# Attention steps rebuilt: head norm's inverse root on POOL, scaling behind the next squares, new order at group changes and ends

## The reference, cut to what matters

```python
def sliding_window_attention(h, positions, w_in, q_gain, k_gain, sinks, w_out):
    q, k, v = split(h @ w_in)                  # 16 heads of q, 4 of k and v, head size 64
    q = rope(rmsnorm(q, q_gain), positions)    # mean square over the 64 of a head, + 1e-6
    k = rope(rmsnorm(k, k_gain), positions)
    # blocks of 128 queries; keys of the block before and of its own
    scores = einsum("bnqkgd,bnskd->bnkgqs", q, k) * 64 ** -0.5
    scores = where(band of 128, scores, -inf)
    probs = softmax(concat([scores, sink]))[..., :-1]
    o = einsum("bnkgqs,bnskd->bnqkgd", probs, v)
    return o @ w_out
```

## Time and profile before

| | us |
|---|---|
| median of 3 runs | 2653.89 |
| lowest, highest | 2653.49, 2654.97 |
| the profiled execution, device time | 2654.76 |
| its span in the trace | 2653.1 |
| TensorE busy | 2569.6 (97%) |
| VectorE busy | 1771.6 (67%) |
| ScalarE busy | 927.8 (35%) |
| POOL busy | 278.2 (10%) |

### The profile page before, as it was taken

How to read it: one execution, slowest core, us unless ns; L and a number is a source line. 1 busy time by engine, 2 the same in 40 slices (tenths; PEclk the granted TensorE clock), 3 DMA queues, 4 the chain that set the end, 5 groups by cost and what they waited for, 6 DMA issues and landing times.

```text
span 2653.1 us, 36828 instructions
## 1 busy us (share of the span) xinstructions
PE 2569.6 (97%) x11929; PEld 2145.0 (81%) x11929; DVE 1771.6 (67%) x3397; ACT 927.8 (35%) x1732; POOL 278.2 (10%) x344
## 2 busy tenths in 40 slices
PE   8999999999999999999999978988999999999999
PEld 6888878888788888888888867877877888888887
DVE  6545454454577876667766777888878666667765
ACT  5332332323311544442111255545554444311112
POOL 2102011020000300000000052322330000000000
PEclk9999999999999999999999999999999999999999
DMA  6012120121433333353233201001023323532332
GB/s 202 31 51 69 48 74 14 48 72 48 143 96 99 123 116 123 103 177 124 95 96 101 82 21 41 17 24 40 17 76 115 127 96 110 206 96 95 95 97 85
DMA packets 161729, 231.67 MB, mean 87 GB/s; under 512 B 21681, under 2 KB 103889, under 8 KB 161618
## 3 DMA queue, kind: packets, MB, share of 16 engines
q1 hardware_dynamic: 159314, 226.10, 26.5%
q10 hardware_dynamic: 2304, 4.20, 0.4%
HBM read 171.53 MB, written 58.73 MB: 87 GB/s over the span
## 4 chain that ended last, share of the span: by engine, by line
PE 80%; DVE 10%; issue 5%; ACT 4%; DMA 1%; POOL 0%; SPq 0%; DVEq 0%; ACTq 0%; POOLq 0%
PE ps L480 26%; PE ps L482 26%; PE ps L481 26%; ACT xn L1936 2%; DVE smax L1982 1%; DVE hss L2015 1%; DVE pT_lo L1960 1%; PE ps L1362 0%; PE ps L1313 0%; PE ps L1345 0%; DVE xT L659 0%; PE ps L1315 0%; PE ps L1314 0%; DVE ws_lo L1806 0%; DVE hT_lo L531 0%
## 5 line engine op out<-in xcount | busy, mean ns | idle before, releaser
L659 DVE TENSOR_TENSOR xT<-ps,xT 128x512 f32<-128x512 f32 x704 | 482.2, 689 | 264.1 <-PE ps L482 263.9
L480 PE MATMUL ps<-aT_hi,wd_hi 128*128 128x512 f32 x1408 | 554.0, 393 | 23.6 <-DVE xT L659 19.6
L482 PE MATMUL ps<-aT_hi,wd_lo 128*128 128x512 f32 x1408 | 550.3, 391 | 0.0
L481 PE MATMUL ps<-aT_lo,wd_hi 128*128 128x512 f32 x1408 | 550.0, 391 | 0.0
L480 PE MATMUL ps<-bh,uw_hi 128*128 128x512 f32 x880 | 343.7, 391 | 6.8 <-DVE xn L857 6.0
L481 PE MATMUL ps<-bl,uw_hi 128*128 128x512 f32 x880 | 343.3, 390 | 0.0
L482 PE MATMUL ps<-bh,uw_lo 128*128 128x512 f32 x880 | 343.1, 390 | 0.0
L480 PEld LDWEIGHTS ps<-aT_hi,wd_hi 128*128 128x128 f32 x1408 | 265.5, 189 | 78.7 <-DVE xT L659 14.4
L482 PEld LDWEIGHTS ps<-aT_hi,wd_lo 128*128 128x128 f32 x1408 | 265.4, 189 | 55.9
L481 PEld LDWEIGHTS ps<-aT_lo,wd_hi 128*128 128x128 f32 x1408 | 265.8, 189 | 53.7
L442 ACT ACTIVATE aT_hi<-raw 128x1024 fp32r<-128x1024 f32 x80 | 80.6, 1052 | 595.7 <-PE ps L482 580.7
(11 more groups left out here) (287 smaller groups left out, 4649.0 us busy)
## 6 DMA issues: line engine op xcount, KB each, us to landing
raw<-in_w_up SPq DMA_DIRECT2D x64, 512.0 KB, 5.6
raw<-in_w_down SPq DMA_DIRECT2D x64, 512.0 KB, 3.6
raw<-a_dram SPq DMA_DIRECT2D x64, 512.0 KB, 3.3
raw<-in_ret_w_in SPq DMA_DIRECT2D x48, 512.0 KB, 5.0
a_dram<-upost SPq DMA_DIRECT2D x64, 256.0 KB, 2.1
a_dram<-xn SPq DMA_DIRECT2D x64, 256.0 KB, 2.0
xT<-x_dram SPq DMA_DIRECT2D x24, 512.0 KB, 6.0
y_dram<-xn SPq DMA_DIRECT2D x32, 256.0 KB, 2.3
```

The costliest lines, as they stand in the source:

```text
L480: pe.matmul(bank, ah, bh, start=(begin and i == 0), stop=False, skip_group_check=not begin)
L481: pe.matmul(bank, ah, bl, start=False, stop=False, skip_group_check=not begin)
L482: last = pe.matmul(bank, al, bh, start=False, stop=(i == len(pairs) - 1), skip_group_check=not begin)
L659: dve.tensor_tensor(xT[:, k, cols], ps[:, banks[m % len(banks)], :], xT[:, k, cols], ALU.add).then_inc(x_add, 1)
```

## The change

It has six parts.

1. The head norm's inverse root: VectorE works out the seed in one operation (L479); the refinement, ten operations on 128x5 (`rsqrt_rest`), runs on POOL between the gains and the rotation. The constant factors are folded into the scale of the mean. VectorE's scaling of the heads waits for the tenth; the maxima and the sink stand behind it. All other inverse roots have eight operations for nine.
2. `prob_act` has lag 2 instead of 1 and stands behind `sq_act`.
3. The turn: TensorE runs f0 and f1 ahead of a; VectorE's two additions of the turn come first in it; b of a group's last block waits for them (`ahead = 2`). In the step before the turn the additions and masks are mixed with the splits, and all stand ahead of the scaling.
4. The start: one tile of the down projection fewer is left between the steps, a of the first block waits for the norm's low parts piece by piece, POOL adds its norm parts elsewhere.
5. The end: in the drain ScalarE scales block 6 first, and the edges of the norm (`b_hi_act`, `edge_low`) all stand in the drain.
6. The inverse root of the last norm's second half stands ahead of a split of MLP weights instead of behind it (`plain_dve`, with `p_hi_act` to match), and that of the attention's norm is worked out between other work in step 3 of group 0.

```diff
-RSQ = 9
+RSQ = 8
+REST = 10
+HSCALE = (256 / 3) ** 2
+HCONST = (3.0, 20 / 3, 320 / 9)
...
+        def rsqrt_seed(dve, a, r):
+            return dve.tensor_scalar(r.bitcast(I32), a.bitcast(I32), -0.5, float(0x5F3759DF), ALU.mult, ALU.add)
+
+        def rsqrt_rest(pool, count, base, a, r, t):
+            def step(k, ins):
+                ins.then_inc(count, 1)
+                pool.wait_ge(count, base + k + 1)
+            step(0, pool.tensor_tensor(t, r, r, ALU.mult))
+            step(1, pool.tensor_tensor(t, t, a, ALU.mult))
+            step(2, pool.tensor_tensor(t, hconst[:, 0, :], t, ALU.subtract))
+            step(3, pool.tensor_tensor(r, t, r, ALU.mult))
...
+            step(9, pool.tensor_tensor(r, t, r, ALU.mult))
...
-        FILLED = TILES - 3
+        FILLED = TILES - 2
...
             if layer == 1:
-                p_lo_dve(dve, layer, 7)
                 norm_rstd(dve, 3, 0)
             for kk in range(4):
                 t_dve(dve, layer, 6, kk)
+            if layer == 1:
+                p_lo_dve(dve, layer, 7)
...
+            if isinstance(g, int) and i == 0:
+                for k in range(KT):
+                    pe.wait_ge(n_lo, TILES + k + 1)
+                    last = product(pe, ps[:, SA, 0:SW_COLS], pairs[k:k + 1], begin=k == 0)
...
+            ahead = 2 if t == TT - 1 and not (isinstance(g, int) and g == SW_KV - 1) else 0
             if not isinstance(i, int) or i > 5:
-                pe.wait_ge(x_add, TILES * DG_SW + 2 * (i - 5))
+                pe.wait_ge(x_add, TILES * DG_SW + 2 * (i - 5) + ahead)
...
             pool.tensor_tensor(qk_raw[:], qk_raw[:], qkgain[:], ALU.mult).then_inc(sw_gain, 1)
+            pool.wait_ge(sw_var, 3 * (i + 1))
+            rsqrt_rest(pool, sw_rsq, REST * i, hvar[:], hrs[:], htmp[:])
...
         def drain_act(act, s):
             if s == TT:
+                prob_act(act, LAST, TT - 2)
...
-                for t in (2, 3):
+                for m in (4, 5):
+                    add(dve, DG_SW + LAST, m, BDS)
+                for t in range(4):
                     edge_low(dve, 1, t)
                 p_lo_dve(dve, 1, 0)
-                for m in (4, 5):
-                    add(dve, DG_SW + LAST, m, BDS)
...
                     if turn:
                         run(lambda *a: f_pe(*a, 0), g, s, FLAG)
+                        run(lambda *a: f_pe(*a, 1), g, s, FLAG)
                     a_pe(eng, g, s)
...
                     sq_act(eng, g, s)
+                    run(prob_act, g, s, 2)
                     run(qkT_act, g, s, 1)
...
                     run(oT_act, g, s, 2)
-                    run(prob_act, g, s, 1)
...
-                        work = lows(g, s) + splits[:2] + masks[:2] + splits[2:] + masks[2:]
+                        work = lows(g, s) + outs[:1] + scores[:2] + splits[:1] + outs[1:] + splits[1:]
+                        outs = []
                     else:
-                        work = lows(g, s) + masks
-                    scale_dve(eng, g, s, work)
-                    for w in out_adds(g, s):
+                        work = lows(g, s) + scores[:2]
+                    for w in work:
                         w()
+                    scale_dve(eng, g, s)
+                    for w in scores[2:] + outs:
+                        w()
```

More of the change, by code:

```diff
@@ L461, in step @@
                 dve.wait_ge(count, base + k + 1)
[L463 to L467, removed]
-            c = math.sqrt(3 / 8)
@@ L470, in rsqrt @@
[L470 to L473, removed]
+            step(0, rsqrt_seed(dve, a, r))
+            step(1, dve.scalar_tensor_tensor(t, r, -0.5, r, ALU.mult, ALU.mult))
+            step(2, dve.tensor_tensor(t, t, a, ALU.mult))
+            step(3, dve.scalar_tensor_tensor(r, t, 1.5, r, ALU.add, ALU.mult))
@@ L1037, in plain_act @@
                 h12_act(act, layer, kk, final)
[L1038 to L1045, removed]
+            for i in (5, 6):
+                for kk in range(4):
+                    b_hi_act(act, layer, i, kk, final)
+            p_hi_act(act, layer, 7)
             for s in range(3):
@@ L1816, in a_pe @@
                     pe.wait_ge(x_add, TILES * DG_SW - 3)
-            if isinstance(g, int) and g == 0 and t % 4 == 0:
-                hT_ready(pe, t // 4)
+            if isinstance(g, int) and g == 0 and t == 4:
+                hT_ready(pe, 1)
             wait(pe, sw_vlo, i)
-            product(pe, ps[:, SA, 0:SW_COLS],
-                    [(hT_hi[:, k, t * P:(t + 1) * P], hT_lo[:, k, t * P:(t + 1) * P], ws_hi[:, k, :], ws_lo[:, k, :])
-                     for k in range(KT)]).then_inc(a_mm, 1)
+            pairs = [(hT_hi[:, k, t * P:(t + 1) * P], hT_lo[:, k, t * P:(t + 1) * P], ws_hi[:, k, :], ws_lo[:, k, :])
+                     for k in range(KT)]
+            if isinstance(g, int) and i == 0:
+                for k in range(KT):
+                    pe.wait_ge(n_lo, TILES + k + 1)
+                    last = product(pe, ps[:, SA, 0:SW_COLS], pairs[k:k + 1], begin=k == 0)
+                last.then_inc(a_mm, 1)
+            else:
+                product(pe, ps[:, SA, 0:SW_COLS], pairs).then_inc(a_mm, 1)
         def b_pe(pe, g, t):
@@ L2131, in drain_act @@
             if s == TT:
+                prob_act(act, LAST, TT - 2)
                 qkT_act(act, LAST, TT - 1)
                 pT_act(act, LAST, TT - 2)
-                for kk in (2, 3):
+                act.wait_ge(a_mm, TT * SW_KV)
+                for kk in range(4):
                     b_hi_act(act, 1, 1, kk, SW_FINAL)
@@ L2240, in step @@
                     run(c_pe, g, s, 1)
-                    run(lambda *a: f_pe(*a, 1), g, s, FLAG)
+                    if not turn:
+                        run(lambda *a: f_pe(*a, 1), g, s, FLAG)
                     run(e_pe, g, s, 2)
@@ L2264, in step @@
                     run(oT_act, g, s, 2)
-                    run(prob_act, g, s, 1)
                     if begins and s == 1:
-                        for m in (FILLED + 1, FILLED + 2):
+                        for m in (FILLED, FILLED + 1):
                             last_norm_act(eng, m)
[L2269 to L2272, removed]
                 if which == "dve":
-                    if begins and s == 1:
-                        fill_dve(eng, FILLED)
+                    outs = out_adds(g, s)
+                    if turn:
+                        for w in outs:
+                            w()
+                        outs = []
                     run(qkT_dve, g, s, 1)
@@ L2298, in step @@
                     if begins and s < 3:
-                        for m in ((8, 9, 10), (11, 12), (13, 14, 15))[s]:
+                        for m in ((8, 9, 10), (11, 12, 13), (14, 15))[s]:
                             norm_low(eng, m)
-                    if begins and s == 3:
-                        norm_rstd(eng, 2, 1)
-                    if last_group and s == TT - 1:
-                        for m in range(2):
-                            edge_low(eng, 1, m)
                 if which == "pool":
                     rope_sw_pool(eng, g, s)
-                    if begins and s < 2:
-                        norm_pool(eng, 2, 1, ((3,), (4, 5, 6, 7))[s])
+                    if begins and s == 1:
+                        norm_pool(eng, 2, 1, (6, 7))
             def group(g, last_group):
@@ L2573, in _ @@
                 pool.memset(flat if z is kr else flat.bitcast(F32), 0.0).then_inc(sw_zero, 1)
+            for j, c in enumerate(HCONST):
+                pool.memset(hconst[:, j, :], c).then_inc(sw_zero, 1)
             norm_pool(pool, 2, 0)
-            norm_pool(pool, 2, 1, (1, 2))
+            norm_pool(pool, 2, 1, (1, 2, 3, 4, 5))
             sw_steps("pool", pool)
```

42 lines of the change are left out of this document (30 added, 12 removed).

## The result

The changed kernel took 2673.49 us in the median of 4 runs (2672.24 to 2675.66), the kernel before 2653.99 (2653.49 to 2654.97, 4 runs): ratio 1.0074, 95% interval 1.0056 to 1.0091. It is slower by 19.5 us. The profiled execution took 2672.24 us with a span of 2670.6, which is 17.5 us more than the span before.

A forecast was written before the change was run, and what follows sets the result against it. Two loops, TensorE's and one through VectorE and ScalarE, both turned at 11.35 us a step. Terms 1.9 + 21.3 - 8.1 + 3 - 5 = +13.1 on 2654.76, less 0.87, gave 2667 us; range 2651 to 2687.

The forecast's parts named there:

- Steady step: Seven of a group's eight steps: 12.3 us each, 0.93 more; +21.3 us over 21 steps of groups 1 to 3.
- the second loop: Loop through VectorE and ScalarE, vp_lo to vp_lo: 9.3 us plus POOL's chain, 12.3 us; TensorE's loop is the other, 12.2.
- POOL's price: Ten small head-norm operations in a row on POOL: 3.0 us taken, ends 2.6 and 3.8.
- Turn: Three turns between groups: vp_lo to vp_lo falls from 20.71 to 18.0 us, b starting at 16.0; -8.1 us for three.
- Start: Kernel start together with group 0's steps (+5.5 us): +1.9 us.
- -3.6: Start without group 0's steps: the 2.9 us wait for hT_lo goes and a(0) gains some 0.7 us.
- Drain: After the last vp_lo: late maxima lengthen VectorE's chain, last d at 26.2 us instead of 24.2; +3 us, ends +1 and +4.5.
- Last norm: Behind the attention: inverse root fits into VectorE's idle 4.36 us ahead of the split, all behind comes sooner; -5 us.
- Hidden scaling: Rival: ScalarE's scaling ends beside b, so d is not held; steps stay 11.36 us, total 2640 us; chance 0.12.
- Turns close: Rival: b never waits, TensorE keeps full clock, turns under 15 us; total 2652 us, half of it 2659; chance 0.14.
- Slow POOL: Rival: POOL's chain in each step takes 3.8 us, steps 13.0 us; total about 2686 us; chance 0.17.
- stretched case: POOL's chain stretched by 1.7 beside VectorE's work to 5 us, giving 2710 us.

The follow-up runs named there:

- the kernel without the two edits: Changed kernel with the root back on VectorE, its operations one by one between other work, and ScalarE's scaling back at the step's end: 2639.87 us.

## Why the prediction was right, and where it was off

- **Steady step, right, with two sizes off that cancelled.** d came 1.46 us behind a's end (1.43 said), steps took 12.25 us (12.3), 21.4 us in all (21.3). With the scaling put back the second loop alone gave 12.68 us for 12.7 worked out, and with the root put back the first alone 12.21. On VectorE sdif's end at 6.84 us behind vp_lo met the 6.8 by luck: the chain took 2.68 us where the sum has 3.0, so L2056 came 0.3 us sooner than said, and the three small operations took 0.71 us, from 1899.22 to 1899.93, where the sum has 0.4. The 21.4 us too hold one step of 13.80 (see the end) that no term forecast.
- **POOL's price, right at its lower end.** 0.20 us for 128x5 is the value of the line through the larger shapes, and 2.68 us for the chain lies near the 2.6 of the range. No operation of the chain was stretched: in all 32 blocks it took 2.67 to 2.72 us, beside P^T's low halves, masks and additions. The splits of weights, which the rule in the prediction names, stood behind it and never met it. What was stretched is VectorE's: the sink's two small operations took 0.22 and 0.40 us beside POOL's rotation (1899.22, 1899.47), and 0.16 and 0.17 without it, at 1896.10 and 1896.30 in the kernel with both put back. The rule of the Trainium skill ("SBUF — State Buffer", who interferes with whom), that a VectorE instruction with two SBUF inputs shares a port with GpSimd, agrees with the first; for the second, the same section names tensor_scalar among the operations that can take the shared pair.
- **Turn, half right: -4.4 for -8.1.** The step that failed is "b at 16.0, vp_lo at 18.0" for all three. In the first turn b started 16.2 us behind vp_lo and the next vp_lo came 2.1 behind b, as said: 18.27 us. In the third b came at 16.3 and vp_lo 2.5 behind it: 18.78. The extra 0.4 is TensorE's clock behind b's wait. In the first turn b's first two transposes took 0.44 us at a granted clock of 0.94 (1652 to 1653), in the third 0.66 at 0.50, the lower of the two levels, 1.2 GHz (1866.1 to 1867.1). The prediction has this half clock as an end of its range but priced it at nothing in its sum. In the second turn the same half clock came on top of 2.31 us in which VectorE stood still ahead of the additions: 21.13. In the trace of before a wait of this kind could cost nothing, because VectorE idled 7.59 us there anyway, until ScalarE's high parts came:

```profile
1753.32 0.42 DVE L1953 TENSOR_TENSOR qT_lo<-ps,qT_hi 128x256 fp32r<-128x256 f32 x1 [7.59 <-ACT kT_hi L1921]
```

  The change put the additions, which b waits for, directly behind the jump. With them ahead of it the wait is gone, and without them the next work behind the jump has it; that it is the jump's own time is the reading of this, not a row. L2056 at 8.06 us behind vp_lo met the 8.1 said partly by luck: two additions stand ahead of it and the prediction counted one, while its 0.3 us for handovers did not come.
- **Start, half right: +3.9 for +1.9.** "-3.6" was mis-sized: the first vp_lo came 2.24 us sooner (1547.90, now 1545.66). The wait for hT_lo did go, and a(0) began at 1537.50 instead of 1540.52. But then its squares waited for the inverse root of the norm, which the prediction has nowhere. POOL's norm work, over at 1539.83 in the kernel before, now runs to 1543.65 beside that root, and two of VectorE's operations in it took 1.20 us each, where they took 0.16:

```profile
1541.04 1.20 DVE L469 TENSOR_TENSOR rtmp<-rtmp,var 128x4 f32<-128x4 f32 x1
...
1544.37 0.53 ACT L1924 ACTIVATE scr<-ps,rstd 128x320 f32<-128x320 f32 x1 [2.86 <-DVE rstd L476]
```

  The steps of group 0 gave +6.2 (+5.5 said).
- **Drain, right:** +3.1 for +3. The last d came 25.7 us behind the last vp_lo (26.2 said, 24.2 before); the other 1.6 us are behind it, where the granted clock was 0.50 from 1980.7 to 1983.7 and 1.00 in that place before. **Last norm, right:** 5.3 us by the experiment for 5; 1.2 us more came with what stands around it.
- **Rivals.** "Hidden scaling" had 2640 us for steps of 11.36: that is what the kernel without the two edits took, 2639.87, but by taking them out. "Turns close" needed turns under 15 us; the shortest of any run is 15.87. "Slow POOL" needed a chain of 3.8 us. Its stretched case of 5 us does not give 2710: two us more in each of 27 steps make 2721.
- **The total.** 2667 was said and 2673.49 measured. 4.4 us of the 6.5 are the parts above, the turn and the start less what the last norm gave more. The rest is how the profiled executions lie to their medians: 0.87 us above in the kernel before, 1.25 below in the changed one.

## What to carry to other kernels

Write down each loop that closes over a step, engine by engine, with its length: two loops of equal length hide each other. In the steps where both bind, an edit that shortens one is worth nothing, and one that lengthens either costs in full. Work taken off a busy engine onto an idle one is no gain if it was interleaved there and stands in a row here: ten operations hidden between long ones cost some 1 us on VectorE and 2.7 us on POOL in front of everything that waits. Try the parts of a large change apart; here the kernel without two of its parts was 34 us faster (2639.87 against 2673.49), and these two hid what the others brought. Put nothing that another engine waits for directly behind a loop's jump, or look in the trace what stands still there (2.3 to 2.4 us here).

## What I had not expected of the hardware

Beside POOL's norm work of four 128x512 operations, which lasted 6.12 us, VectorE's `tensor_tensor` and `scalar_tensor_tensor` of 128x4 took 1.20 us twice and 0.16 us between.

Behind a wait of some 2.2 us TensorE's clock sometimes fell and sometimes did not, within one execution. Two steps behind a turn in the changed kernel, d waiting 2.28 and 2.21 us; the columns are start and end, length, busy us of TensorE, its weight loads, VectorE, ScalarE and POOL, granted clock, DMA share, GB/s:

```profile
1664.50:1672.50 8.00, 7.31 (x32) 6.14 (x33) 5.84 (x14) 2.78 (x8) 3.47 (x12) 0.79 0.00 0
```

```profile
1773.60:1781.60 8.00, 7.32 (x43) 6.60 (x44) 6.70 (x15) 2.77 (x8) 4.37 (x14) 1.00 0.00 0
```

The first of these steps took 13.80 us, the second 12.46. The waits of the turns show the same: behind 3.56 us b began at full clock and fell to 0.50 within a microsecond, behind 3.64 us it began at 0.50. The changed kernel's trace has two steps of 13.8 us, that with the norm put back three, that with d behind f0 none, which may be why the runs of one kernel lie some 3 us apart; that was not tried.
